# Seven block products in place of eight in block 2's first FFN product, with weight sums made by accumulating DMAs

## The reference, cut to what matters

```python
def squared_relu_mlp(x, w1, w2):
    h = jnp.square(jax.nn.relu(jnp.einsum('bsd,df->bsf', x, w1)))
    return jnp.einsum('bsf,fd->bsd', h, w2)

def second_block(x, mem, positions, ...):
    for l in range(DEPTH):                       # DEPTH = 2
        ...
        x = layer_norm(ALPHA * x + cross, ln2_g[l], ln2_b[l])
        ff = squared_relu_mlp(x, w_ff1[l], w_ff2[l])
        x = layer_norm(ALPHA * x + ff, ln3_g[l], ln3_b[l])
```

## Time and profile before

| | us |
|---|---|
| median of 3 runs (2855.74 to 2856.23) | 2856.2 |
| span of the profiled execution, first to last instruction | 2853.0 |
| median less the span | 3.2 |
| PE busy in it | 2772.6 (97%) |
| DVE busy | 1639.5 (57%) |
| ACT busy | 1267.9 (44%) |
| POOL busy | 403.3 (14%) |

### The profile page before, as it was taken

The page is one execution under the profiler, slowest core; times in us unless marked ns, Lnnn a source line. Parts: engine busy times, 40 slices in busy tenths (PEclk is TensorE's granted clock), DMA queues, the critical chain, the costliest instruction groups (busy, mean ns, idle before and its releaser), DMA issues.

```text
span 2853.0 us, 39111 instructions
## 1 busy us (share of the span) xinstructions
PE 2772.6 (97%) x15784; PEld 2353.1 (82%) x15784; DVE 1639.5 (57%) x2465; ACT 1267.9 (44%) x2133; POOL 403.3 (14%) x305
## 2 busy tenths in 40 slices
PE   9999999999989999999999999999999999999997
PEld 8878999999877788887668888888776688888886
DVE  6776545454777745454876466333658764753335
ACT  5674322224674422233564545333445644443333
POOL 2222000001222000001333120000313331200003
PEclk9999999999999999999999999999999999999999
DMA  4112232232112233332123223333222232233322
GB/s 153 45 45 67 89 97 85 94 92 83 49 45 74 93 96 97 102 93 89 56 75 126 88 67 96 98 95 96 85 82 63 75 126 81 67 104 96 96 96 67
DMA packets 71923, 244.35 MB, mean 86 GB/s; under 512 B 9153, under 2 KB 10817, under 8 KB 71745
## 3 DMA queue, kind: packets, MB, share of 16 engines
q1 hardware_dynamic: 67392, 237.28, 26.4%
q10 hardware_dynamic: 4352, 4.58, 0.5%
HBM read 239.73 MB, written 2.10 MB: 85 GB/s over the span
## 4 chain that ended last, share of the span: by engine, by line
PE 86%; DVE 8%; ACT 4%; issue 2%; POOL 0%; DMA 0%; ACTq 0%; DVEq 0%; SPq 0%
PE psum L589 24%; PE psum L595 24%; PE psum L592 24%; PE psum L661 2%; PE psum L684 1%; PE psum L688 1%; PE psum L686 1%; PE psum L922 1%; PE psum L1095 1%; PE psum L1107 1%; PE psum L950 1%; PE psum L939 1%; PE psum L975 1%; DVE weights_hi_lo L1766 1%; PE psum L778 1%
## 5 line engine op out<-in xcount | busy, mean ns | idle before, releaser
L589 PE MATMUL psum<-act_hi_lo,weights_hi_lo 128*128 128x264 f32 (+2 forms) x2544 | 777.6, 345 | 3.7 <-ACT temp L1300 2.8
L592 PE MATMUL psum<-act_hi_lo,weights_hi_lo 128*128 128x264 f32 (+2 forms) x2544 | 752.2, 335 | 1.9 <-DVE weights_hi_lo L1766 1.9
L595 PE MATMUL psum<-act_hi_lo,weights_hi_lo 128*128 128x264 f32 (+2 forms) x2544 | 753.4, 335 | 0.0
L1196 ACT ACTIVATE weights_hi_lo<-weights_float 128x1024 fp32r<-128x1024 f32 (+2 forms) x446 | 463.6, 1042 | 499.8 <-PE psum L595 430.6
L1766 DVE TENSOR_TENSOR weights_hi_lo<-weights_float,weights_hi_lo 128x1024 fp32r<-128x1024 f32 (+2 forms) x432 | 540.7, 1252 | 219.0 <-ACT weights_hi_lo L1196 217.8
L589 PE MATMUL psum<-hidden_hi_lo,weights_hi_lo 128*128 128x512 f32 (+2 forms) x1584 | 520.2, 358 | 3.7 <-DVE x_residual L2020 1.4
L595 PE MATMUL psum<-hidden_hi_lo,weights_hi_lo 128*128 128x512 f32 (+2 forms) x1584 | 512.2, 353 | 1.4 <-DVE hidden_hi_lo L2030 1.4
L592 PE MATMUL psum<-hidden_hi_lo,weights_hi_lo 128*128 128x512 f32 (+2 forms) x1584 | 511.8, 353 | 1.3 <-DVE weights_hi_lo L1766 1.3
L589 PEld LDWEIGHTS psum<-act_hi_lo,weights_hi_lo 128*128 128x128 f32 x2544 | 440.5, 189 | 68.1 <-issue 17.7
L595 PEld LDWEIGHTS psum<-act_hi_lo,weights_hi_lo 128*128 128x128 f32 x2544 | 439.3, 189 | 47.9
L592 PEld LDWEIGHTS psum<-act_hi_lo,weights_hi_lo 128*128 128x128 f32 x2544 | 438.7, 189 | 47.7 <-issue 2.6
(11 more groups left out here) (294 smaller groups left out, 3343.0 us busy)
## 6 DMA issues: line engine op xcount, KB each, us to landing
weights_float<-in_w_ff SPq DMA_DIRECT2D x128, 512.0 KB, 3.6
weights_float<-in_w_gu SPq DMA_DIRECT2D x88, 512.0 KB, 3.6
weights_float<-in_w_in SPq DMA_DIRECT2D x70, 512.0 KB, 3.7
weights_float<-in_w_down SPq DMA_DIRECT2D x32, 448.0 KB, 3.3
weights_float<-in_w_out SPq DMA_DIRECT2D x16, 512.0 KB, 3.6
weights_float<-in_w_down SPq DMA_DIRECT2D x16, 512.0 KB, 3.5
weights_float<-in_w_mv SPq DMA_DIRECT2D x16, 512.0 KB, 3.3
weights_float<-in_w_mix SPq DMA_DIRECT2D x16, 512.0 KB, 3.5
```

Of the source, the lines that this page charges most:

```text
L589: e.matmul(slot[:, place:place + c1 - c0], w_hi[:, col], x_hi[:, c0:c1], start=first, stop=False)
L592: e.matmul(slot[:, place:place + c1 - c0], w_lo[:, col], x_hi[:, c0:c1], start=False, stop=False)
L595: mm = e.matmul(slot[:, place:place + c1 - c0], w_hi[:, col], x_lo[:, c0:c1], start=False, stop=final)
L1196: e.activation(K.parts(n)[0][:, 0:cols], K.staged(n)[:, 0:cols], ACT.Copy).then_inc(*K.did("hi", n))
```

## The change

Groups 1 to 3 of a layer (hidden tiles 8 to 31) no longer make their first product tile by tile. Two tiles, a pair, are seen as a 2 x 2 block matrix: weights of tile f and of tile f+1, each cut into input chunks 0 to 3 and 4 to 7, by tokens cut into 0 to 255 and 256 to 511. Such a product of 2 x 2 blocks takes eight block products; by a scheme of sums (Strassen's, in Winograd's form) it takes seven, here called forms. A form is 4 chunks x 3 matmuls of 256 tokens: 12 matmuls. A group is 4 pairs (`FORM_PAIRS`), 28 forms (`FORMS`); there are three such groups in each of two layers, 24 pairs.

- The forms need sums of token blocks. DVE makes them once a layer, in group 0 (`sums`: 16 subtractions or additions of 128 x 256), ACT and DVE split them (16 each), and they are kept in a part of the arena.
- The forms need sums of weight blocks. SP loads four halves of pieces (128 x 512, 256 KB each) per pair into half staging buffers, called chains 0 to 3. POOL then issues DMAs that add another half piece from HBM onto what stands in the staging buffer (`accum_op=ALU.add`): one onto chain 0, one onto chain 1, three onto chain 3, 5 a pair, 120 in the program. An add may only go out when the splits of what stood there before are done. Of form j (0 to 6) of a pair, `FORM_CHAIN` names the chain and `FORM_SUMS` how many adds it must have had: form 4 needs chain 1's add, form 5 chain 0's, form 3 the second and form 6 the third add of chain 3.
- Every form's weights are split by ACT and DVE, 128 x 512 at a time, 6 forms ahead: when form m has ended, form m+6 is split (slot m below is the place in ACT's or DVE's program behind the wait for form m). The last slots of a group split `w_ff2`'s first pieces instead: slots 23, 25 and 27 (`FORMS_PARTS`). SP may load the first of these pieces once form 27 is split (`FORMS_STAGING`), which happens in slot 21.
- The forms' results must be combined. ACT copies form 0's result before form 2 is accumulated onto the same bank (`first`), form 1's before form 5 is (`third`), and the sum of forms 0 and 2; DVE adds and subtracts blocks of 128 x 256 (`outer`, `inner2`, `upper`, `upper2`, `lower`). PE waits for `first` ahead of form 2, for `third` ahead of form 5, for `inner2` ahead of form 6. The odd tile's relu and square stay with ACT, the even tile's are one DVE instruction (`squared`).
- The second product takes hidden chunk 7 before chunk 6. Some semaphores are shared by more names, SBUF addresses move by 1024 bytes (`LINE_PAD`, `dynamic_dma_scratch_size`).

```diff
+FORM_BANK = (0, 1, 0, 2, 3, 1, 3)
+FORM_BEGINS = (True, True, False, True, True, False, False)
+FORM_CHAIN = (0, 1, 2, 3, 1, 0, 3)
+CHAIN_HALF = ((0, 1, 2, 3), (4, 1, 2, 5))
+FORM_SUMS = (0, 0, 0, 2, 1, 1, 3)
+FORMS_PARTS = [23, 25, 27]
+FORMS_STAGING = [27, 25, 23]
...
+def tensor_forms(e, w, K, B, l, f0):
+    did, done = K.did, K.done
+    for p in range(FORM_PAIRS):
+        banks = [4 * (p % 2) + b for b in range(4)]
+        for j in range(7):
+            m = 7 * p + j
+            b, adds = banks[FORM_BANK[j]], not FORM_BEGINS[j]
+            if FORM_BEGINS[j]:
+                B.clear(b)
+            if j == 2:
+                w.wait_ge(*done("first", l, f0, p))
+            if j == 5:
+                w.wait_ge(*done("third", l, f0, p))
+            if j == 6:
+                w.wait_ge(*done("inner2", l, f0, p))
+            w_hi, w_lo = K.form_parts(l, f0, m)
+            w.wait_ge(*done("form_hi", l, f0, m))
+            for k in range(DC // 2):
...
@@ in scalar_block2, ACT's program @@
+    def forms(f0):
...
+            w.wait_ge(*done("form", l, f0, m))
+            if j == 0:
+                if p > 0:
+                    w.wait_ge(*done("outer", l, f0, p - 1))
+                e.activation(K.first, X, ACT.Copy, scale=-1.0).then_inc(*did("first", l, f0, p))
...
+            if m + 6 < FORMS:
+                split_form_hi(e, w, K, l, f0, m + 6)
+            elif m in FORMS_PARTS:
+                split_hi(e, w, K, PIECE["w_ff2", l, FORMS_PARTS.index(m), f0, f0 + 8])
+            if j == 6:
+                w.wait_ge(*done("upper2", l, f0, p))
+                e.activation(raised(f + 1), raised(f + 1), ACT.Relu).then_inc(*did("relu", l, f + 1))
+                square(f + 1)
+                hidden_high(f + 1)
+                if p == FORM_PAIRS - 1:
+                    hidden_high(f)
+            if j == 0 and p > 0:
+                hidden_high(f - 2)
...
@@ in pool_forms, POOL's program @@
+    long(0, 1)
+    long(0, 2)
+    for p in range(FORM_PAIRS):
+        split(7 * p)
+        add(p, 0, 1, 1, 0)
+        split(7 * p + 1)
+        add(p, 1, 1, 1, 0)
+        long(p + 1, 1)
+        split(7 * p + 3)
+        add(p, 3, 3, 0, 1)
+        long(p + 1, 2)
...
@@ in sync_program, SP's loads @@
+        after = K.after_forms(n)
+        if after is not None:
+            l, f0, i = after
+            w.wait_ge(*done("form_hi", l, f0, FORMS_STAGING[i]))
+            w.wait_ge(*done("form_lo", l, f0, FORMS_STAGING[i]))
```

More of the change, by code:

```diff
@@ L112 @@
     norm_stat=("qk_stat", "sub_stat", "rec_stat", "sq_stat", "mean_sum", "shift_sum"),
+    bias=("far", "near"), lam_exp=("lsig_exp",), mean=("mean_square",), conv_first=("conv2_first",), cube=("gelu_tanh",),
+    hi=("form_hi",), lo=("form_lo",), product=("form",),
+    relu=("first", "third", "relu_first", "sum_hi"), corrected=("sum", "sum_lo", "outer", "inner2", "upper", "upper2", "lower", "squared"),
+    landed_x0=("landed_chain1",), landed_x1=("landed_chain3",), landed_x2=("landed_chain5",),
+    landed_weights0=("landed_chain0",), landed_weights1=("landed_chain2",), landed_weights2=("landed_chain4",),
     hid_hi=("hid_hi2", "gx_hi", "gx_columns_hi"), hid_lo=("hid_lo2", "gx_lo", "gx_columns_lo"),
@@ L300, in pieces @@
         for f0, f1 in FF2_GROUPS:
-            order += [("w_ff1", l, f) for f in range(f0, f1)]
+            order += [("w_ff1", l, f) for f in range(f0, f1)] if f0 == 0 else [("forms", l, f0), ("forms_end", l, f0)]
             order += [("w_ff2", l, n, f0, f1) for n in range(DC)]
@@ L377, in rings @@
         for f0, f1 in FF2_GROUPS:
-            keys += [("w_ff1", l, f) for f in range(f0, f1)]
+            keys += [("w_ff1", l, f) for f in range(f0, f1)] if f0 == 0 else []
             keys += [("w_ff2", l, f0, n) for n in range(DC)] if f1 < FF2_TILES else normed("w_ff2", l)
@@ L452, in __init__ @@
         self.mq = arena[:, qbase:qbase + DC * T2].rearrange("p (n t) -> p n t", n=DC)
+        at = EARLY * T2 + 2 * 4 * DC // 2 * HALF
+        self.first, self.third, self.outer, self.inner2 = (arena[:, at + n * HALF:at + (n + 1) * HALF] for n in range(4))
         self.psum = m["psum"]
@@ L1613, in scalar_normed_chunk @@
         if k == 0:
-            w.wait_ge(*done("product", LN_FREE[name, l]))
+            w.wait_ge(*(done("form", l, FF2_FIRST[-1], FORMS - 1) if name == "w_ff2" else done("product", LN_FREE[name, l])))
         e.activation(out(k, T2)[0], tmp, ACT.Identity, bias=shift, scale=gain).then_inc(*did("in_hi", name, l, k))
@@ L2466, in vector_block2 @@
     for f0, f1 in FF2_GROUPS:
-        for f in range(max(f0, EARLY), f1):
+        if f0 > 0:
+            forms(f0)
+        for f in range(EARLY, f1 if f0 == 0 else 0):
             if f == EARLY:
@@ L2477, in vector_block2 @@
         alpha = ALPHA if f0 == 0 else 1.0
+        if f0 == 0:
+            for k in range(DC // 2):
+                sums(k)
         if f1 < FF2_TILES:
@@ L2628, in pool_block2 @@
     pool_normed(e, w, K, l, "w_mo", SHIFT_TILES)
+    for f0 in FF2_FIRST[1:]:
+        pool_forms(e, w, K, l, f0)
     pool_normed(e, w, K, l, "w_ff2")
@@ L2654, in load, with load_forms @@
         e.dma_start(K.staged(n)[:, 0:src.shape[-1]], src).then_inc(*did(LANDED[n % STAGING], n, by=16))
+    def load_forms(l, f0):
+        for p in range(FORM_PAIRS):
+            for chain in (0, 3, 2, 1):
+                half, before = K.chain_name(l, f0, p, chain), chain_before(p, chain)
+                if before is not None:
+                    w.wait_ge(*done("form_hi", l, f0, before))
+                    w.wait_ge(*done("form_lo", l, f0, before))
+                else:
+                    w.wait_ge(*done("hi", PIECE["forms", l, f0] - STAGING + half // 2))
+                    w.wait_ge(*K.low(PIECE["forms", l, f0] - STAGING + half // 2))
+                tile, part = ((0, 0), (1, 1), (0, 1), (0, 0))[chain]
+                e.dma_start(K.chain(l, f0, p, chain), t["w_ff1"][l, f0 + 2 * p + tile, :, part * FORM:(part + 1) * FORM]).then_inc(
+                    *did(f"landed_chain{half}", l, f0, p, chain, by=16))
     for c in range(DC):
```

222 lines of the change are left out of this document (201 added, 21 removed).

## The result

The changed kernel takes 2945.9 us (median of 4 runs, 2944.4 to 2951.4) where the kernel before takes 2856.0 in the same session (4 runs, 2854.2 to 2856.2): ratio 1.0313, 95% interval 1.0301 to 1.0325. It is slower by 3.1%, far above the forecast of 2850 and above the whole range.

The account below looks back on a forecast made before the run. PE's own pace was taken as the bound, with room on everything else. From 2856.2 us, 19.2 saved on matmuls and 12.6 added for a late `w_ff2` load gave 2849.6, say 2850; range 2841 to 2888.

Parts of the forecast that it names:

- What PE saves: First product: a pair's matmuls fall from 10.88 to 10.08 us; 0.80 a pair, 24 pairs, -19.2 us.
- The token sums: DVE's and ACT's small instructions in group 0, 48 a layer, hidden beside other work: taken as 0.
- The price of an add: Issue to landing of POOL's adding DMA, not in the trace: taken as 3.4 us, between plain DMAs of 3.2 and 3.6.
- place 1: ACT's `first` ahead of form 2, behind a split that waits for chain 1's add: on the edge, no stall.
- the bounds, 2.3 and 5.9: Limits in us on an add: a plain 128 KB DMA below, 3.6 plus a second transfer's fixed part above.
- I am wrong if an add takes over 4 us: Sign named beforehand that would refute the forecast: an add's time above 4 us.
- So the add may take 3.4 us: Time allowed from issue to landing before slot 5's split makes `first` late: from 6.2 to 9.6 us.
- At 5.9 the 12 places ... 2.5 each, 30 us: 2880: Cost if adds take the upper 5.9 us: `first` late by 2.5 us in 12 places, 30 us, total 2880.
- Start of a group ... 0: Six forms split under `w_ff2`'s last three tiles, chain loads going out 20 us ahead: no cost, 0.
- place 2: Last pair: PE waits for `inner2` behind a low part of late-loaded `w_ff2`; 2.1 us in six groups, +12.6 us.
- The DMA engines or POOL become the bound (2878): Rival: a pair's loads and adds need 11.65 us, 1.57 more than PE, in 18 pairs: 28.3 us; chance 0.35.
- the adds are late at place 1 (2859): Rival: chain 1's add lands late behind chain 0's, 0.9 us in 12 places, 10.8 us; chance 0.20.

Follow-up runs that it names:

- sums_ahead: Changed kernel with weight sums built in HBM during block 1's feed-forward, seven plain halves loaded a pair, ACT's odd-tile high part behind `first`: 2841.8 us, ratio 0.9943.
- no_adds: Changed kernel without its 120 adding DMAs, every form's weights taken from the plainly loaded half: 2869.9 us, ratio 1.0037.
- chains_0_1_warm: adds_of_chains_0_1 plus 20 matmuls of no use ahead of PE's wait for `first` in a group's pairs 2 to 4: 2917.7 us, ratio 1.0201.
- adds_of_chains_0_1: Changed kernel without chain 3's three adds a pair (72 of 120 left out): 2923.1 us, ratio 1.0227.
- plain_copies: Changed kernel with POOL's 120 DMAs copying the same bytes in place of adding: 2890.9 us, ratio 1.0109.
- no_adds_late_lows: no_adds with DVE's low parts of `w_ff2`'s first three pieces in slots 25, 26 and 27, behind `inner2` and `upper`: 2854.9 us, ratio 0.9984.

## Why the prediction was wrong

- **What PE saves: right.** Matmuls 0.120 us apart, a pair 10.08 us where nothing waits (sums_ahead), groups 84.07 against 87.04, so 2.97 of 3.2. The token sums cost nothing: from 1700 to 1790 us PE is busy 87.8 us before and after.
- **"The price of an add ... I take 3.4, midway between the two nearest rows, and so no stall at place 1": this step failed.** The sum had 0 for this stall and PE waited 63.8 us. An add measured 5.1 us, and chain 1's, the one in question, 5.5. Both rows were plain DMAs on other queues; the bounds, 2.3 and 5.9, held the median, and the value was chosen from inside them so that it fell on the edge of a stall, with nothing but symmetry for it. The sign "I am wrong if an add takes over 4 us" came true.
- **The price alone does not make the miss.** At 5.1 the prediction's own formula gives 12 x 1.7 = 20 us, 2870, inside the range. What a late add costs was wrong as well, by the next three points. An add of 5.5 and 7.6 us of engines make a turn of 13.1 against 10.08, so 3.0 in each of 18 places, 54 us. From `first` to `first` the 18 turns are on average 10.2 us in sums_ahead, 10.5 in no_adds, 13.7 in chains_0_1_warm, 14.0 in adds_of_chains_0_1 and 14.7 in the changed kernel: most is chain 1's loop, and the rest is chain 3's adds and the half clock.
- **"So the add may take 3.4 us": also off.** The rest of the loop came out at 7.6 us and not 6.7. It lacks POOL's issue of chain 0's add, 0.53 ahead of chain 1's, and DVE's two hidden low parts (1.2 us), which stand between DVE's splits of slot 0 and of slots 1 and 2; they send the way round through DVE where the prediction had it through ACT, so that the loop grows by 0.9 and not by both. plain_copies shows it with a DMA of the 3.4 us that were allowed: pairs of 11.2.
- **"At 5.9 the 12 places ... 2.5 each, 30 us: 2880": the upper bound was too low.** It has 12 places, the second and third pair of a group; but the fourth follows a full slot 6 too, and waited 20.0 us in six groups. And "Start of a group ... 0" hid 8.0 us in the first pairs of two groups. So the waits were 20, of 3.2 us on average and not 2.5, and the clock comes on top. Even the end of the range, 2888, near that bound of 2880, missed by 58 us.
- **The clock was not in the sum at all**, though every wait counted there was one ahead of matmuls. In the changed kernel it is 37 to 39 us by the account, and at place 2, measured alone, 1.7 for a wait of 2.1. How much of the 37 to 39 would come back with the clock is open; in chains_0_1_warm the mean clock rose by 0.7% of the span, 20 us, and 7 us came back, with intervals that overlap.
- **Place 2: right** in place, mechanism and size (2.1 forecast and 2.2 measured in no_adds, 12.6 and 13.0 in all), but for the clock behind it, and the cure named there, DVE's block ahead, removes it. With the adds it shrinks to 7.9, since `first` has already held PE up.
- **The rival "the DMA engines or POOL become the bound (2878)"**: its price of an add was right, 1.66 against 1.67 us, and its mechanism was not. The DMA share in the first product is 0.73 on average, with slices at 0.99, and loads and adds that need only 6.6 us of engine time a pair still give 1.0227. That traffic delays landings (of chain 1's adds from 3.9 to 5.5 us) is what is left of it. Its range, 2862 upward, held the measured time, and had 0.35; that it did so by another mechanism is luck.
- **The rival "the adds are late at place 1 (2859)"** was the right mechanism, the second of two adds issued together landing later (by 1.6 us at the median in adds_of_chains_0_1, where it had 0.7), at a sixth of its size: 10.8 us against 63.8. Its own sum comes to 2860.

Open: how much of the growth of a landing from 3.9 (the quickest) to 7.8 us is the add just ahead and how much the loads beside it; whether chain 1's add issued ahead of chain 0's would help, which no run tried; and some 2 us of no_adds_late_lows.

## What to carry to other kernels

Before a transfer that changes a buffer in place is put between two uses of it, write out the loop that it closes, one turn, every instruction of every queue that it passes, with its issue; the loop's length against the work of a turn decides, not the busy share of any engine. Where the price of the new leg has no row, price the loop at the upper bound and give that case the weight that ignorance deserves; a value in the middle of the bounds that just avoids the stall is no finding. A wait of PE of about two microseconds cost nearly as much again by its clock where nothing else closed a loop (1.7 for 2.1, no_adds) and far less where a loop set the pace (chains_0_1_warm); ask first which of the two a wait is. And move work that depends on nothing new (here sums of constants) to a stretch where the engines that make it are idle and nobody waits.
